# Half of the later conditioning vectors of a two-block transformer made on TensorE, in halves between FFN steps, instead of on VectorE

## The reference

```
cond = silu(c)
for l in range(DEPTH):
    m = (cond @ w_mod[l] + b_mod[l]).reshape(bsz, 3, 3, D_MODEL)
    x = x + 0.5 * m[:, 0, 2] * swiglu(adaln_in(x, norm_g[l, 0], m, 0), w1, w3, w2)
    h = adaln_in(x, norm_g[l, 1], m, 1) @ w_in[l]
    mix = mixer_ab(h, ...) if l % 2 == 0 else mixer_cd(h, ...)
    x = x + m[:, 1, 2] * (mix @ w_out[l])
    x = x + 0.5 * m[:, 2, 2] * swiglu(adaln_in(x, norm_g[l, 2], m, 2), w1, w3, w2)
# adaln_in(x, g, m, i) = rmsnorm(x, g) * (1 + m[:, i, 1]) + m[:, i, 0]
```

## Time and profile before

| | before |
|---|---|
| median of 3 runs | 1641.95 us (1640.35 to 1642.67) |
| the profiled execution: its own time | 1640.37 us |
| its span in the profile | 1638.6 us |
| mean granted TensorE clock | 0.956 of full |
| DMA | 420.31 MB, mean 257 GB/s |
| PE, DVE, ACT busy | 89%, 83%, 60% |

### The profile page before, as it was taken

One profiled execution on the slowest core, in us unless ns is written; L12 is line 12 of the kernel. 1 busy time (PEld: TensorE's weight loads), 2 busy tenths in 40 slices (PEclk: granted clock), 3 DMA queues, 4 the chain that ended last, 5 costly groups with the idle time before them and its releaser, 6 DMA issues.

```text
span 1638.6 us, 27675 instructions
## 1 busy us (share of the span) xinstructions
PE 1460.2 (89%) x11160; PEld 1375.4 (84%) x11160; DVE 1361.1 (83%) x2231; ACT 982.0 (60%) x1640; POOL 81.9 (5%) x153
## 2 busy tenths in 40 slices
PE   7989758798979888887999999999999999988997
PEld 4888657697969786766998998987999899868997
DVE  2999758899999999877888988686988888687886
ACT  4555536555566446545676766547766766577665
POOL 0113010001101110000000000000000000000000
PEclk9999979899999999998999999899999999799999
DMA  9999563679968994427886877334777677435773
GB/s 387 366 385 415 204 235 140 251 289 333 392 237 323 402 395 155 154 77 284 284 317 227 281 276 262 123 148 170 267 273 272 231 276 278 162 116 199 274 273 129
DMA packets 84972, 420.31 MB, mean 257 GB/s; under 512 B 9363, under 2 KB 9795, under 8 KB 58094
## 3 DMA queue, kind: packets, MB, share of 16 engines
q1 hardware_dynamic: 64478, 343.48, 57.7%
q0 software_dynamic: 20368, 75.06, 12.1%
HBM read 417.38 MB, written 1.13 MB: 255 GB/s over the span
## 4 chain that ended last, share of the span: by engine, by line
PE 41%; DVE 6%; ACT 3%; DMA 2%; issue 1%; DVEq 0%
PE pw L626 13%; PE pw L627 13%; PE acc L626 6%; PE acc L627 6%; DVE low_p L1953 2%; DMA land_d<-stream 1%; ACT h_hi L1358 1%; PE acc L905 1%; PE pw L863 1%; ACT hi_p L1456 1%; ACT sq L1361 0%; PE acc L885 0%; DMA land_p<-stream 0%; ACT hi_d L1456 0%; DVE low_d L1953 0%
## 5 line engine op out<-in xcount | busy, mean ns | idle before, releaser
L626 PE MATMUL pw<-h_hi,hi_p 128*128 128x256 f32 x2976 | 754.3, 292 | 49.8 <-DVE low_p L1953 27.1
L627 PE MATMUL pw<-h_lo,low_p 128*128 128x256 f32 x2976 | 742.9, 288 | 0.0
L626 PEld LDWEIGHTS pw<-h_hi,hi_p 128*128 128x128 f32 x2976 | 587.1, 197 | 69.3 <-issue 30.1
L627 PEld LDWEIGHTS pw<-h_lo,low_p 128*128 128x128 f32 x2976 | 587.3, 197 | 0.4 <-issue 0.2
L1953 DVE SCALAR_TENSOR_TENSOR low_p<-hi_p,land_p 128x1024 fp32r<-128x1024 f32 x418 | 506.8, 1221 | 42.4 <-ACT hi_p L1456 42.1
L1456 ACT ACTIVATE hi_p<-land_p 128x1024 fp32r<-128x1024 f32 x418 | 434.0, 1047 | 64.4 <-DMA land_p<-stream 64.3
L626 PE MATMUL acc<-a_hi,hi_d 128*128 128x256 f32 x1376 | 343.2, 287 | 47.0 <-DVE low_d L1953 35.5
L627 PE MATMUL acc<-a_lo,low_d 128*128 128x256 f32 x1376 | 339.4, 284 | 0.0
L626 PEld LDWEIGHTS acc<-a_hi,hi_d 128*128 128x128 f32 x1376 | 265.4, 193 | 54.9 <-issue 41.1
L627 PEld LDWEIGHTS acc<-a_lo,low_d 128*128 128x128 f32 x1376 | 265.7, 193 | 0.0
L1953 DVE SCALAR_TENSOR_TENSOR low_d<-hi_d,land_d 128x1024 fp32r<-128x1024 f32 x205 | 249.4, 1218 | 11.7 <-ACT hi_d L1456 11.6
(11 more groups left out here) (354 smaller groups left out, 1665.7 us busy)
## 6 DMA issues: line engine op xcount, KB each, us to landing
land_p<-stream SPq DMA_DIRECT2D x207, 1024.0 KB, 5.1
land_d<-stream SPq DMA_DIRECT2D x209, 512.0 KB, 5.6
modw<-wmod POOLq DMA_DIRECT2D x116, 512.0 KB, 8.5
biasT<-wmod POOLq DMA_DIRECT2D x12, 512.0 KB, 4.2
biasT<-bias_rows POOLq DMA_DIRECT2D x3, 1536.0 KB, 11.4
modw<-wmod SPq DMA_DIRECT2D x8, 512.0 KB, 7.6
biasT<-wmod SPq DMA_DIRECT2D x8, 512.0 KB, 10.7
biasT<-bias_rows POOLq DMA_DIRECT2D x1, 3072.0 KB, 13.5
```

What stands on the lines that cost most here:

```text
L626: mm(o, lhs[0], rhs[0], start=start, stop=False, skip_group_check=True)
L627: return mm(o, lhs[1], rhs[1], start=False, stop=stop, skip_group_check=True)
```

## The change

It makes eight of the 16 later vectors (5, 6, 7, 10, 11, 14, 15, 16) on PE. Each is made in two halves of four blocks, so 16 halves: six in stage 0, four in stage 2, six in stage 3. `STREAMED` says ahead of which step's `up` a half is summed (`half_sums`: 8 products in four column tiles, into `pssq`). ACT copies the row out (128 x 512, after that step's `a_hi`), PE turns it behind the `up` of the next step (`half_turn`: four products of one column), and DVE adds the bias (`half_total`). The loads of the halves are issued by SP, four of 0.5 MB into four buffers in `biasT`, each after the products that used the buffer for the half before. DVE keeps the vectors 2, 3, 4, 8, 9, 12, 13, 17 (`SUMMED`), 24 blocks in stage 0, 16 in stage 2, 16 in stage 3, 8 in stage 5, and none in the `ab` mixer. The filter's layers and taps of stage 2 move to earlier steps. `w_mod` is laid out for the halves beforehand.

```
-MOD_AT = {0: [[]] + spread(2, 7, 20, 4) + [[]], 2: [[]] * 3 + spread(8, 12, 17) + [[]] * 2,
-          3: [[]] * 3 + spread(12, 17, 17) + [[]] * 2, 5: [[]] * 3 + spread(17, 18, 18) + [[]]}
+MOD_AT = {0: [[]] + spread(2, 5, 20) + [[]], 2: [[]] * 3 + spread(8, 10, 17) + [[]] * 2,
+          3: [[]] * 3 + spread(12, 14, 17) + [[]] * 2, 5: [[]] * 3 + spread(17, 18, 18) + [[]]}
...
+SUMMED = (2, 3, 4, 8, 9, 12, 13, 17)
+STREAMED = {0: {2: (5, 0), 5: (5, 1), 8: (6, 0), 11: (6, 1), 14: (7, 0), 17: (7, 1)},
+            2: {14: (10, 0), 16: (10, 1), 18: (11, 0), 20: (11, 1)},
+            3: {4: (14, 0), 7: (14, 1), 10: (15, 0), 13: (15, 1), 16: (16, 0), 19: (16, 1)}}
...
+    before = 0.5
+    for i in sorted(STREAMED):
+        for j, which in STREAMED[i].items():
+            freed.append((max(before, 3 * FIRST[i] + 0.4) if HALF_NO[which] else before, "mod", which))
+            before = 3 * (FIRST[i] + j) + 0.2
...
-LAYER_AT, TAP_AT = (3, 6, 9), (12, 13, 14, 15)
+LAYER_AT, TAP_AT = (3, 5, 7), (9, 10, 11, 12)
...
+            def load_half(g, h):
+                x = HALF_NO[g, h]
+                if (g, h) == (10, 0):
+                    sp.wait_ge(triple_used, FIRST[2])
+                for n in range(4):
+                    sp.wait_ge(mod_taken, 2 * KD + 4 * (x - 1) + n + 1)
+                    sp.dma_start(streamed_slot(n), wmod[g, 4 * h + n]).then_inc(half_load[n], 16)
...
+                    if j in STREAMED.get(i, {}):
+                        half_sums(*STREAMED[i][j])
...
+                    if j - 1 in STREAMED.get(i, {}):
+                        half_turn(*STREAMED[i][j - 1])
...
+            def half_sums(g, h):
...
+                for n in range(4):
+                    pe.wait_ge(half_load[n], 16 * (x + 1))
+                    for u in range(2):
+                        kc = n * 2 + u
+                        q = kc % 4 * 32
+                        m = mm(pssq[q:q + 32, :], condz[:, kc, :], streamed_slot(n)[:, u * 512:(u + 1) * 512],
+                               start=(kc < 4), stop=(kc >= 4), skip_group_check=True)
+                    m.then_inc(mod_taken, 1)
...
+            def half_turn(g, h):
+                pe.wait_ge(half_copied, HALF_NO[g, h] + 1)
+                for c in range(4):
+                    m = mm(pssq[:, c:c + 1], mod_row[:, c * P:(c + 1) * P], ones[:, 0:1], start=(c == 0), stop=True, skip_group_check=True)
+                m.then_inc(half_turned, 1)
...
+                if j in STREAMED.get(i, {}):
+                    act.wait_ge(mod_taken, 2 * KD + 4 * HALF_NO[STREAMED[i][j]] + 4)
+                    fn(mod_row[:], pssq[:], ACT.Copy).then_inc(half_copied, 1)
...
+            def half_total(g, h):
+                o = PAR_AT["bmod"][0] + g * KD + 4 * h
+                dve.wait_ge(half_turned, HALF_NO[g, h] + 1)
+                v.tensor_tensor(modT[:, g, 4 * h:4 * h + 4], pssq[:, 0:4], par_s[:, o:o + 4], ALU.add).then_inc(half_read, 1)
...
-                mods_ab(3)
...
-                mods_ab(2)
...
-                mods_ab(8, 1)
```

More of the change, by code:

```diff
@@ L126, in spread @@
     return [blocks[cut[s]:cut[s + 1]] for s in range(slots)]
-MOD_AT = {0: [[]] + spread(2, 7, 20, 4) + [[]], 2: [[]] * 3 + spread(8, 12, 17) + [[]] * 2,
-          3: [[]] * 3 + spread(12, 17, 17) + [[]] * 2, 5: [[]] * 3 + spread(17, 18, 18) + [[]]}
+MOD_AT = {0: [[]] + spread(2, 5, 20) + [[]], 2: [[]] * 3 + spread(8, 10, 17) + [[]] * 2,
+          3: [[]] * 3 + spread(12, 14, 17) + [[]] * 2, 5: [[]] * 3 + spread(17, 18, 18) + [[]]}
 RAW = (2, 3, 5)
-MOD_FIRST = {min(some[0] for some in MOD_AT[i] if some): i for i in (2, 5)}
-_ab = iter([(6, k) for k in range(4, KD)] + [(7, k) for k in range(KD)])
-MOD_AB = {(back, b): [next(_ab) for _ in range(count)] for back, b, count in AB_MODS}
+SUMMED = (2, 3, 4, 8, 9, 12, 13, 17)
+STREAMED = {0: {2: (5, 0), 5: (5, 1), 8: (6, 0), 11: (6, 1), 14: (7, 0), 17: (7, 1)},
+            2: {14: (10, 0), 16: (10, 1), 18: (11, 0), 20: (11, 1)},
+            3: {4: (14, 0), 7: (14, 1), 10: (15, 0), 13: (15, 1), 16: (16, 0), 19: (16, 1)}}
+MOD_FIRST = {(8, 0): 2, (17, 0): 5}
+HALF_NO = {half: n for n, half in enumerate(half for i in sorted(STREAMED) for half in STREAMED[i].values())}
 def load_groups():
@@ L283, in mod_slot, with streamed_slot @@
             if g < 2 and k >= MODR:
[L284 to L287, removed]
+                return streamed_slot(k - MODR)
+            return modw[:, (k if g < 2 else SUMMED.index(g) * KD + k) % MODR, :]
+        def streamed_slot(n):
+            return biasT[:].rearrange("p h c -> p (h c)")[:, 2048 + n * D:2048 + (n + 1) * D]
         h = proj[:, 0:KD, :]
@@ L383, in build @@
         mod_load = [sem(f"mod_load{i}") for i in range(2 * MODR)]
+        half_load = [sem(f"half_load{i}") for i in range(MODR)]
+        half_copied, half_turned, half_read = sem("half_copied"), sem("half_turned"), sem("half_read")
         mod_late = [sem(f"mod_late{i}") for i in range(MODR)]
@@ L533, in _ @@
                     for what, which in LOADS[i, n]:
-                        if what == "pair":
+                        if what == "mod":
+                            load_half(*which)
+                        elif what == "pair":
                             load_pair(which)
@@ L565, in load_mods @@
             def load_mods(first, last):
-                for n in range(first, last):
-                    g, k = n // KD, n % KD
-                    if n < 2 * KD + MODR:
+                for m in range(first, last):
+                    g, k = SUMMED[m // KD], m % KD
+                    if m < MODR:
                         pool.wait_ge(mod_taken, 2 * KD)
                     else:
-                        held = 2 if 6 * KD + 4 <= n < 8 * KD else MODR
-                        pool.wait_ge(mod_used, n - 2 * KD - held + 1)
+                        pool.wait_ge(mod_used, m - MODR + 1)
                     if (g, k) in MOD_FIRST:
                         pool.wait_ge(triple_used, FIRST[MOD_FIRST[g, k]])
-                    pool.dma_start(mod_slot(g, k), wmod[g, k]).then_inc(mod_late[k % MODR], 16)
+                    pool.dma_start(mod_slot(g, k), wmod[g, k]).then_inc(mod_late[m % MODR], 16)
             o1, o2 = PAR_AT["ng1"][0], PAR_AT["ng2"][0]
@@ L2063, in gated @@
                     v.tensor_tensor(act_in[0:r, j % 2, :], sig[0:r, j % 2, :], up_half, ALU.mult).then_inc(gated_ready, 1)
+                    if j - 1 in STREAMED.get(i, {}):
+                        half_total(*STREAMED[i][j - 1])
                     if smooth(i, j) and j < NFF - 1:
@@ L2671 @@
     wmod = np.ascontiguousarray(a["w_mod"].reshape(2, D, 9, KD, P).transpose(0, 2, 3, 4, 1).reshape(NMOD, KD, P, D)[FIRST_SCALE])
-    for g in range(FIRST_MODS):
+    for g in list(range(FIRST_MODS)) + sorted({g for g, _ in HALF_NO}):
         rows = wmod[g].reshape(D, D).T.reshape(4, 2, P, 2, 512)
```

43 lines of the change are left out of this document (27 added, 16 removed).

## The result

The changed kernel takes 1657.93 us in the median of 4 runs (1654.3 to 1659.74), beside 1641.15 us for the kernel before in its 4 runs. The ratio is 1.0098 [1.0079, 1.0118]: slower by 1%, where 0.8% faster was forecast, and outside the range. The profiled execution, the slowest of the four, took 1659.74 us, its span 1658.0 (before 1638.6).

A forecast was written before the change was run, and what follows sets the result against it. PE was taken to bound the plain FFN, DVE stages 0, 2 and 3 (stage 0 also DMA), a chain of waits `ab`. +8 - 15 - 3.9 - 2.4 = -13.3 us from 1641.95 gives 1628.6 us, range 1612 to 1643.

The forecast's parts named there:

- DVE: Sums removed from stages 0, 2, 3 leave DVE 114, 117 and 104 us busy, below what PE needs.
- PE per half: Each half summed on PE adds 3.4 us (2.7 to 5), including 0.55 for the switch to full width.
- Stage 3: PE's floor 113.7 plus six halves gives 134.1 us against 136.45: -2.4 us (-6.6 to +7).
- Stage 2: PE's floor, four halves and the filter give 134.8 us against 138.74: -3.9 us (-7 to +3).
- Stage 0: Added bytes, 58.4 MB in all, lengthen the stage by +8 us (+2.4 to +13.6).
- `ab`: Without DVE's sums the mixer loses waits in its middle and at its end: -15 us (-20 to -9).
- A: Rival: stage 0 is not bound by bytes and takes PE's 136 us; total -22.3, 1619.6 us; chance 0.20.
- B: Rival: weights land late behind halves in stages 2 and 3, +25 us; total 1653.7 us; chance 0.14.
- C: Rival: the waits of `ab` belong to weights, not sums; total -3.8, 1638.2 us; chance 0.10.
- D: Rival: memory gives less; stage 0 at 342 GB/s takes 171 us, +33; total 1654 us; chance 0.03.
- Sum: All terms together for the whole kernel: -13.3 us, giving 1628.6 us; chance 0.53.

The follow-up runs named there:

- e2: The kernel before with only the filter's steps moved (layers 3, 5, 7, taps 9 to 12), no half on PE: 1658.51 us, ratio 1.0106.
- e10: The changed kernel with other step numbers for filter and halves in stage 2 alone, and the waits these need: 1638.3 us, ratio 0.9969.
- e9: e7 with stage 2's halves at steps 10, 16, 18, 20 and the taps at 12 to 15: 1629.81 us, ratio 0.9916.
- e3: The changed kernel with each load of a half in stage 0 cut from 1024 to 128 columns: 1638.75 us, ratio 0.9973.
- e6: e5 with stage 0's first half loads issued later and its halves at steps 5, 8, ..., 20: 1638.74 us, ratio 0.9984.
- e7: e6 with the four loads of a half issued half a step apart and two large constant loads cut into four: 1637.91 us, ratio 0.9977.
- e8: The kernel before with the twelve sums of `ab` done by DVE in stage 0, nothing on PE: 1661.96 us, ratio 1.0129.
- e1: The changed kernel with the filter's layers three steps apart (2, 5, 8) and taps at 11 to 14: 1644.36 us, ratio 1.0009.
- e5: e1 with the halves of stage 2 ahead of steps 9, 15, 17, 19, and waits to match: ratio 1.0001.

## Why the prediction was wrong

The step that failed is in the part on stage 2: "Moving the filter's steps forward changes nothing else: DVE has the room." Room was the wrong question. e2 shows that moving them costs 15.4 us on the kernel before, and e10 that placing them well gives 18.0 back. What the step overlooked is the path from a layer on PE over DVE's reduction and ACT's sine to the next layer on PE. DVE's part stands at the end of its step, and ACT's at the end of the step after, each behind that step's other work in an in-order queue. So PE finds the sine ready three steps later and not two, whatever the busy shares are. At two steps PE waited 4.0 us three times in the kernel after, and 14.6 us in all in e2; at three it waited 0.7 at most. The earlier trace rows only shows the price of a tap that had its three steps. The prediction named no rival for it.

Term by term:

- **DVE.** Right: 115, 118 and 105 us busy, where 114, 117 and 104 were worked out.
- **PE per half.** 2.8 us, not 3.4; the bounds held. The 0.55 us read at the start for the switch of the tile size doesn't recur: in the stream both switches of the sums come to 1.95 - 1.74 = 0.2 us. What the rest of the 0.55 was isn't shown. The Trainium skill (TensorEngine Tiling (Array Packing), Key Properties) says that a switch of the tiling mode drains the engine; no row shows the drain by itself, only this price. Stage 3 as a whole gives (131.44 - 113.7) / 6 = 3.0 us per half in e9 and 3.6 in the kernel after.
- **Stage 3.** -1.2 us against -2.4; -5.0 in e9, within the bounds, as the spread of this stage (131.4 to 135.6 us over the runs) is.
- **Stage 2.** With the filter well placed it takes 138.89 (e10) and 137.40 (e9) against the forecast's 134.8. So -3.9 was 2.6 to 4.1 us too good, the wrong placement apart. The sum took PE for busy throughout. In e9 it is busy 133.69 us, near the 134.8, and idle 3.7, and 3.5 of these are waits at `pssq`: 2.0 for a half's total on DVE, 0.7 for DVE's reading of a tap, 0.8 for loads of halves. The floor of 113.7 was low as well: the same stage 5 took 115.1 to 117.0 us in the eleven other profiles.
- **Stage 0.** The mechanism was right (e3: 15 of 17 us go with the bytes), the size was not: this is the second term that failed, +17 us for +8. The bytes were 59.0 MB, nearly as counted (58.4). I took the middle between the best rate of an 18 us stretch (418 GB/s) and the mean rate of the stage (387). The mean rate holds: 58.4 MB at 387 give 150.9, and e9 takes 150.00 at 393. The last 2 to 4 us of the kernel after (152.2 to 154.4 over four profiles of this stage) can be bursts ahead of weight pairs, of which e6 and e7 together remove 2.6. The term to take was the upper end.
- **`ab`.** -18 us against -15, the same in e8 (-17.6). DVE no longer awaits `w_mod` there, PE's waits of 5.41 and 6.56 us are 0.69 and 0.66, the 7.31 us behind the mixer are 2.76, and the residual starts before PE is done. (The low bound of -9 doesn't follow from the prediction's own terms: the end, 5.5, and half of the middle, 4.5, are 10.) DVE's timeline:

```profile
296.91 0.88 DVE L2075 SCALAR_TENSOR_TENSOR x<-pw,ada,x 128x256 f32<-128x256 f32 x2 [2.56 <-PE pw L649]
```

- **Rivals.** A (stage 0 not bound by bytes) is refuted by e3, and by e9, where the stage has a DMA share of 1.00 for its 150 us. B (weights behind halves) gave 1653.7 us, near the result, but for the wrong reason: the price that e6 and e7 show is some 2.6 us, little more than the spread, and lies in stage 0, not 25 us in stages 2 and 3. C (`ab`'s waits belong to the weights) is refuted by e8. D (memory gives less) gave 1654 and fails too: a whole stage of e9 runs at 393 GB/s. By the 358 GB/s of the Trainium skill (DMA: Bandwidth & Descriptors, Where 436 GB/s comes from), which the section derives by halving the memory's bandwidth between two cores, stage 0 would take 59.0 / 0.358 = 165 us, an estimate; the run, with one core at work, shows 150.
- **Sum.** With the steps of stage 2 alone put right (e10) the change gives 0.31%, 5 us, where 13.3 were forecast. e9 gives 0.84%, 13.8 us of 1644.05, but with the loads' order changed too. That this is near the forecast's -13.3 is luck: it is another kernel, and errors cancel in it (stage 0 +12.7 for +8, `ab` -18 for -15, stage 3 -5.0 for -2.4).

Open: stage 5 takes 115 to 117 us in every variant, also in e2 (115.2), against 113.71 in the one profile of before; nothing in it was changed, and the cause isn't known. The first halves could also be summed by PE inside `ab`, where the DMA share is 0.49; this wasn't tried.

## What to carry to other kernels

When a side computation runs between the steps of a main loop on several in-order engines, its steps must be as far apart as its chain through the queues is long, counted from the order of each engine. Here that is three steps for a layer, whose reduction DVE does at the end of its step and whose sine ACT makes at the end of the next; two steps where PE awaits only the reduction; and one for a tap, which DVE reads at the head of its step. That DVE was busy only 75% of the stage and ACT 50% didn't shorten it. If a change moves such a table of step numbers, cost the table by itself, as one line of it can outweigh the rest. And when bytes were added to a stage that was already at a DMA share of 0.99, its mean rate (387 GB/s) priced them and its best stretch (418) did not.

## What was unexpected of the hardware

A gap on PE costs more than its length. In or behind each gap of 3.2 to 5.6 us that was looked at (in the kernel after, e1, e2 and e5) the granted clock fell to half (1.2 GHz). With PE busy again it stayed there for 3 to 7 us. In e10, where the longest wait in stage 2 is 1.7 us, the mean of the stage is 0.99. The timeline and the stretch of the first half in the kernel after:

```profile
46.54 5.75 PE L1294 MATMUL pssq<-biasT,condz 128*32 128x512 f32 x16 [3.16 <-DMA biasT<-wmod]
```
```profile
46.00:52.00 6.00, 5.46 (x16) 0.76 (x16) 0.10 (x1) 0.00 (x0) 0.00 (x0) 0.50 1.03 421
```

The clock was 0.50 of full throughout, and the half took 5.75 us instead of 1.93. In e1 a half behind a gap took 3.44, so a part of the 5.75 is for its later loads. Stage 2 of the kernel after is 18.0 us longer than that of e10: PE is idle 19.2 us in it instead of 4.6, and busy 137.7 instead of 134.3, for the same work at a mean granted clock of 0.95 instead of 0.99. And changing the tile size of the array and back within a stream of products costs about 0.2 us in all.
